# A four-mixer transformer on one core: orders changed in three stages, decays broadcast through DRAM, one product made transposed

## What is computed

```python
for l in range(2):                      # first block
    x = x + 0.5 * swiglu(rms_norm(x, ffa_norm[l]), ffa_w_in[l], ffa_w_out[l])
    h = rms_norm(x, mix_norm[l])
    (c_q, c_kv, k_rope, g_q, g_k, g_v, g_b, g_a, g_z, m_qkv, gate_logits) = split_cols(h @ w_in[l], IN_SPLITS)
    o_mla, o_gdn, o_moba = mla_branch(...), gdn_branch(...), moba_branch(...)
    x = x + gated sum of the branches @ w_out[l]
    x = x + 0.5 * swiglu(rms_norm(x, ffb_norm[l]), ffb_w_in[l], ffb_w_out[l])
# second block: even_mixer, ffn 0, odd mixer, ffn 1
```

```python
decay = jnp.exp(jnp.where(tril, gcum[..., :, None] - gcum[..., None, :], NEG_INF))
a  = jnp.where(strict, jnp.einsum('bhnid,bhnjd->bhnij', k_beta, k) * decay, 0.0)
qk = jnp.einsum('bhnid,bhnjd->bhnij', q, k) * decay
```

## Time and profile before

| | |
|---|---|
| median of 3 runs | 1898.7 us (1898.09 to 1899.29) |
| profiled execution | 1899.05 us |
| its span, first to last instruction | 1897.2 us |
| granted TensorE clock | 1.000 |
| busy: PE, DVE, ACT, POOL | 1888.0, 1460.1, 1083.3, 82.6 us |
| DMA | 330.87 MB, mean 174 GB/s |
| chain that ended last | PE 93%, DVE 4%, ACT 2% |

### The profile page before, as it was taken

One profiled execution on the slowest core, in us unless ns is written; L12 is line 12 of the kernel. 1 busy time (PEld: TensorE's weight loads), 2 busy tenths in 40 slices (PEclk: granted clock), 3 DMA queues, 4 the chain that ended last, 5 costly groups with the idle time before them and its releaser, 6 DMA issues.

```text
span 1897.2 us, 32403 instructions
## 1 busy us (share of the span) xinstructions
PE 1888.0 (100%) x11807; PEld 1649.0 (87%) x11807; DVE 1460.1 (77%) x2316; ACT 1083.3 (57%) x1683; POOL 82.6 (4%) x61
## 2 busy tenths in 40 slices
PE   9999999999999999999999999999999999999999
PEld 9888998788988888899987888889888889888888
DVE  7777896877777777778778777777578888888887
ACT  6555764664555555567647645555346655775654
POOL 0000011010000000000110010000000000110000
PEclk9999999999999999999999999999999999999999
DMA  6656553445455555555434455565755555545654
GB/s 236 199 189 197 171 188 102 134 152 170 155 190 188 187 186 190 188 183 185 155 112 145 145 172 179 186 197 180 207 179 178 198 189 173 162 143 158 200 186 143
DMA packets 116717, 330.87 MB, mean 174 GB/s; under 512 B 10896, under 2 KB 40208, under 8 KB 116496
## 3 DMA queue, kind: packets, MB, share of 16 engines
q1 hardware_dynamic: 114496, 325.64, 53.2%
q10 hardware_dynamic: 2128, 3.94, 0.6%
HBM read 327.91 MB, written 1.64 MB: 174 GB/s over the span
## 4 chain that ended last, share of the span: by engine, by line
PE 93%; DVE 4%; ACT 2%; DMA 1%; issue 0%; POOL 0%; ACTq 0%
PE ps L2318 89%; DVE w_lo L1319 1%; DMA raw<-stream 1%; PE ps L2344 1%; ACT w_hi L616 1%; PE ps L2617 1%; PE ps L2871 0%; DVE arena L2133 0%; DVE sc L1831 0%; PE ps L3035 0%; PE ps L2812 0%; PE ps L2893 0%; ACT gates L1113 0%; PE ps L2688 0%; DVE tmp L2176 0%
## 5 line engine op out<-in xcount | busy, mean ns | idle before, releaser
L1319 DVE TENSOR_TENSOR w_lo<-raw,w_hi 128x1024 fp32r<-128x1024 f32 x614 | 750.2, 1229 | 223.6 <-ACT w_hi L616 222.5
L2318 PE MATMUL ps<-w_hi,a_both 128*128 128x512 f32 (+2 forms) x2368 | 753.1, 387 | 1.1 <-DVE a_both L2105 0.7
L616 ACT ACTIVATE w_hi<-raw 128x1024 fp32r<-128x1024 f32 x614 | 637.2, 1053 | 160.8 <-DMA raw<-stream 106.0
L2318 PE MATMUL ps<-a_both,w_hi 128*128 128x256 f32 (+1 forms) x3360 | 712.4, 341 | 0.1
L2318 PEld LDWEIGHTS ps<-a_both,w_hi 128*128 128x128 f32 x3360 | 580.7, 190 | 72.8 <-issue 0.8
L2318 PEld LDWEIGHTS ps<-w_hi,a_both 128*128 128x128 f32 x2368 | 441.9, 188 | 88.6 <-issue 1.2
L2318 PE MATMUL ps<-w_lo,a_both 128*128 128x512 f32 (+2 forms) x1184 | 455.4, 385 | 0.0
L2318 PE MATMUL ps<-a_both,w_lo 128*128 128x256 f32 x2592 | 448.1, 283 | 0.0
L2318 PEld LDWEIGHTS ps<-a_both,w_lo 128*128 128x128 f32 x2592 | 380.5, 191 | 8.9
L2318 PEld LDWEIGHTS ps<-w_lo,a_both 128*128 128x128 f32 x1184 | 223.2, 188 | 36.5
L689 ACT ACTIVATE a_both<-arena 128x256 fp32r<-128x256 f32 x132 | 55.2, 419 | 139.4 <-DVE arena L1433 98.7
(11 more groups left out here) (349 smaller groups left out, 1186.7 us busy)
## 6 DMA issues: line engine op xcount, KB each, us to landing
raw<-stream SPq DMA_DIRECT2D x613, 512.0 KB, 3.5
arena<-upad SPq DMA_DIRECT2D x8, 284.0 KB, 6.0
gates<-late ACTq DMA_DIRECT2D x1, 1088.0 KB, 8.7
out<-tmp SPq DMA_DIRECT2D x3, 256.0 KB, 2.3
upad<-arena ACTq DMA_DIRECT2D x2, 288.0 KB, 8.1
con<-consts SPq DMA_DIRECT2D x1, 560.0 KB, 5.1
raw<-stream ACTq DMA_DIRECT2D x1, 512.0 KB, 3.8
x<-x_in ACTq DMA_DIRECT2D x2, 256.0 KB, 5.1
```

What stands on the lines that cost most here:

```text
L616: nc.scalar.activation(laid(w_hi, u), loaded(u), ACT.Copy).then_inc(hi_ready, 1)
L1319: V.tensor_tensor(laid(w_lo, u), loaded(u), laid(w_hi, u), ALU.subtract).then_inc(split_ready, 1)
L2318: return nc.tensor.matmul(o, a, b, start=start, stop=stop, **k)
```

## The change

Mixer, both layers: the running sums are stored to DRAM (1024 runs of 4 bytes) after load moba+1, and read back as 128 rows of 1024 after load moba+4, both on SP's queue; Et reads those rows. "R" is gone from PE. The product is made as K Q^T, masked by a second exponential ET (DVE adds a transposed mask after kgd, ACT takes eight exponentials with the negated sums as bias), so the transposition "QKT" and ACT's copy are gone. z_gate(1) stands between the two reductions, mobars after all of POOL's ATM steps. The constants grow by 128 columns of 1120.

```diff
+            def store_cum(l):
+                sp.wait_ge(*DV.at(l, "cumcp"))
+                sp.dma_start(cumd[l].rearrange("b p -> p b"), sc[:, 72:80], allow_slow_non_contiguous=True).then_inc(cum_stored, 16)
+            def spread_cum(l):
+                sp.wait_ge(cum_stored, 16 * (l + 1))
+                sp.dma_start(flat(rows), cumd[l].rearrange("b p -> (b p)").unsqueeze(0).broadcast_to([PART, 8 * PART])
+                             ).then_inc(cum_spread, 16)
...
+                        if u == POS["moba", l] + 1:
+                            store_cum(l)
+                        if u == POS["moba", l] + 4:
+                            spread_cum(l)
...
+                act.wait_ge(*DV.at(l, "ET"))
+                for b in range(8):
+                    e = nc.scalar.activation(ET[:, b, :], ET[:, b, :], ACT.Exp, bias=sc[:, 280 + b:281 + b])
+                e.then_inc(*AC.sig(l, "ET"))
                 turned_copy(0)
-                act.wait_ge(*PE.at(l, "QKT"))
-                nc.scalar.activation(QKT, ps[:, 4:6, :], ACT.Copy).then_inc(*AC.sig(l, "QKT"))
...
+                        tick(V.tensor_scalar(sc[:, 280:288], bank(6, 0, 8), -1.0, None, ALU.mult))
...
-                dve.wait_ge(*PE.at(l, "R"))
+                dve.wait_ge(cum_spread, 16 * (l + 1))
...
+                for t in range(2):
+                    i = V.tensor_tensor(ET[:, 4 * t:4 * t + 4, :], rows[:, 4 * t:4 * t + 4, :],
+                                        each(const("causalt"), 4), ALU.add)
...
-                ev(DV, "c_lo")
-                for b in range(8):
-                    i = mm(bank(6 + b // 4, 128 * (b % 4), 128 * (b % 4) + 128), sc[:, 240 + b:241 + b].broadcast_to([PART, 128]), const("tri"))
-                i.then_inc(*PE.sig(l, "R"))
...
-                blocks(4, lambda o, tt, h: mm(o, qT(tt, h), kT(tt, h)), "QK")
+                blocks(4, lambda o, tt, h: mm(o, kT(tt, h), qT(tt, h)), "QK")
...
-                ev(DV, "QK")
-                blocks(4, lambda o, tt, h: nc.tensor.transpose(o, QK[:, 4 * tt + h, :], ident), "QKT")
```

```diff
-                split(e0 + AHEAD); split(e0 + 1 + AHEAD)
+                split(e0 + AHEAD)
                 for p in range(2):
                     act.wait_ge(*DV2.at(0, f"yb{p}"))
...
-                split(e0 + 2 + AHEAD)
+                split(e0 + 1 + AHEAD)
...
-                dil_split(4, 5, 6, 7)
+                dil_split(4, 5)
+                nc.scalar.activation(sc[:, 300:301], sc[:, 296:297], ACT.Exp)
+                dil_split(6)
                 dil_evac(1)
                 squares("k", 2)
-                dil_split(8, 9, 10, 11)
+                dil_split(7, 8, 9, 10, 11)
...
+            for j in range(TT):
+                part = slice(DG * DH * j, DG * DH * (j + 1))
+                rsqrt(drs["k"][:, part], dss["k"][:, part]).then_inc(*PO2.sig(0, f"drsk{j}"))
...
                 tile(1, [n0 + 2, n0 + 3])
+                if n0 == POS["ffn", 0]:
+                    decay_rates()
                 with dve.Fori(0, (FT - 4) // 2) as j:
...
-                for i in range(4):
-                    scan = tick(V.tensor_tensor_scan(tqb[:, i, :], aa[:, i, :], thi[:, i, :], 0.0, ALU.mult, ALU.add))
-                dve.wait_ge(*PO2.at(0, "drsk"))
                 for j in range(TT):
+                    dve.wait_ge(*PO2.at(0, f"drsk{j}"))
                     r = dil["k"][:, j, :].rearrange("p (a b) -> p a b", b=DD)
                     e = V.tensor_tensor(r, r, over(drs["k"][:, 12 * j:12 * j + 12], DD), ALU.mult)
                 e.then_inc(*DV2.sig(0, "dk"))
+                for i in range(4):
+                    scan = tick(V.tensor_tensor_scan(tqb[:, i, :], aa[:, i, :], thi[:, i, :], 0.0, ALU.mult, ALU.add))
...
-                    update(t, POS["ffn", i] + 3 * FT, 1.0, ("mix2", 1))
+                    update(t, POS["ffn", i] + 3 * FT, 1.0, ("mix2", 1), between=POS["ffn", i] + 3 * FT - 3 + AHEAD)
```

More of the change, by code:

```diff
@@ L229, in constants @@
         neg += [same, band, same]
+    put("causalt", np.where(causal.T, 0.0, NEG).astype(np.float32))
     put("causal", np.where(causal, 0.0, NEG).astype(np.float32))
@@ L514, in build @@
         wcomp = gr(4592, 4 * TAP_STEP * TAP_GROUPS)
+        rows = reg(11264, 8, PART)
+        cumd = [nc.dram_tensor(f"cumd{l}", (8, PART), F32, kind="Internal").ap() for l in range(DEPTH)]
         upad = nc.dram_tensor("upad", (4 * PART, UPAD), F32, kind="Internal").ap()
@@ L588, in _ @@
                             spread_u(p)
+                    for l in range(DEPTH):
+                        if u == POS["moba", l] + 1:
+                            store_cum(l)
+                        if u == POS["moba", l] + 4:
+                            spread_cum(l)
             for b in range(2):
@@ L1026, in even @@
                 store_u(1)
+                act.wait_ge(*DV2.at(0, "lamz"))
+                link(nc.scalar.activation(sc[:, 288:292], sc[:, 284:288], ACT.Abs))
+                nc.scalar.activation(sc[:, 292:296], sc[:, 288:292], ACT.Exp, scale=-1.0).then_inc(*AC2.sig(0, "spe"))
                 def conv_out(p):
@@ L1067, in even @@
                                          ).then_inc(*AC2.sig(0, f"o2_hi{p}"))
-                for k in range(3, 8):
+                for k in range(2, 8):
                     split(e0 + k + AHEAD)
@@ L2097, in even @@
                 split(e0 + AHEAD)
-                split(e0 + 1 + AHEAD)
                 for p in range(2):
@@ L2106, in even, with decay_rates @@
                                     ALU.subtract).then_inc(*DV2.sig(0, f"o2_lo{p}"))
-                for k in range(2, 7):
+                for k in range(1, 7):
                     split(POS["ev_out"] + k + AHEAD)
+            def decay_rates():
+                dve.wait_ge(*AC2.at(0, "spe"))
+                sp = sc[:, 296:300]
+                log1p(sc[:, 292:296], sp, sc[:, 248:252], sc[:, 256:260], sc[:, 264:268])
+                link(V.scalar_tensor_tensor(sp, sc[:, 284:288], 0.0, sp, ALU.max, ALU.add))
+                V.tensor_scalar(sp, sp, -4.0, None, ALU.mult).then_inc(*DV2.sig(0, "sp4"))
             def odd(t):
```

65 lines of the change are left out of this document (33 added, 32 removed).

## The result

The changed kernel takes 1921.02 us (median of 4 runs, 1915.35 to 1921.32) against 1898.39 us before, measured beside it: ratio 1.0113, 95% interval [1.010, 1.0126]. The forecast was 1894.2 with a range of 1890.0 to 1897.3, so it had the wrong sign. The profiled execution took 1921.02 us with a span of 1919.2, 22.0 us more than before.

The account below looks back on a forecast made before the run. TensorE was taken as the bound, busy 1888.0 of 1897.2 us. Gains of 4.5 (mixer), 0.8 (even), 0.4 (ffn 0's end) and 0.5 (odd) less 1.7 (decay chain) made 4.5 us: 1894.2 us, range 1890.0 to 1897.3.

Parts of the forecast that it names:

- the price of the store: Mixer: the store of the decays to DRAM lands in about 4 us; at most 24.8 us if all cost is per run.
- its first 6.5 us are free: Mixer, SP's queue: source ready at 243.6, spread due near 250, so a store within some 6.5 us delays nothing.
- the slow rival: Mixer: SP waits for the store and holds later loads, DVE and kgd; 1907.2 us with a 14 us store; chance 0.05.
- The row I leaned on: Profile before: a 4 KB load of 128 short runs landed in 3.1 us; basis for the store's 4 us.
- 2.96 - s a layer: Mixer: 2.96 us of removed work and delay less s, PE's new stall for kgd, taken as 0.7 us.
- my signs of being wrong: No stall in ffn 0, both odd waits gone, or ACT waiting several us for loads in the mixer.
- The sentence on the Trainium skill: Mixer's store: runs below 512 bytes are slowest, which would move the sum from 1894.2 towards the rival's 1907.2.
- The mixer's gain, 4.5,: Both mixer layers: 2.25 us gained each, broadcast and transposes gone less a kgd stall; bounds 2.3 to 5.3 us.
- The even stage: Even stage: a weight split moved behind the output activation ends a 0.7 us stall; 0.8 us gained, bounds 0 to 0.9.
- The decay chain: Moved from odd stage to ffn 0's head: PE stalls 1.7 us for a weight split, a loss; bounds 0 to 2.0.
- ffn 0's end: End of ffn 0: x update before the split removes a 0.3 us stall; 0.4 us gained, bounds 0 to 0.5.
- The odd stage: Odd stage: keys scaled before the scans, 0.5 us gained for two stalls; bounds 1.0 lost to 2.9 gained.

Follow-up runs that it names:

- the store alone: Kernel before, with the store of 1024 runs of 4 bytes added on SP's queue and read by nobody: 1913.89 us, ratio 1.0089.
- on another queue (ACT's): Kernel before, with the unused store of 1,024 pieces of 4 bytes issued by ACT on its own DMA queue: 1917.72 us, ratio 1.0101.
- 1,024 pieces apart: Kernel before, with an unused store of all eight columns, each 4-byte piece 512 bytes from the next in DRAM: 1898.31 us, ratio 1.0004.
- the store of one column: Kernel before, with an unused store of one of the 8 columns, 128 pieces of 4 bytes, on SP's queue: 1910.60 us, ratio 1.0064.
- the kernel with 128 runs: The change, with the sums stored in 128 runs of 32 bytes and DVE reading rows with a stride of eight values: 1897.86 us, ratio 1.000.
- the last kernel: The change with 8 stored rows of 512 bytes, decay chain back in odd stage, even stage's last split after x update: 1893.96 us, ratio 0.9981.

## Why the prediction was wrong

**The step that failed** is the price of the store, and with it the reckoning that its first 6.5 us are free. I took 4 us for its landing, "nearest to that row, since a plain load of 512 KB takes 3.5 us too", and gave the slow rival 0.05. It landed in 9.8 and 11.3 us, by the spread that waits for it. The row I leaned on the earlier trace rows was a load of 128 short runs that reads DRAM; a store of short pieces that fill the same stretch is another thing, and no row before had one. My upper bound, eight times that row (24.8 us), was right as a bound but reckoned by the number of runs, and the runs show that the number is not what counts.

**The rival's mechanism was half right.** Its chain, late loads, then DVE, then PE, is what the trace shows. But I let it begin at SP, which waits in order, and so took 6.5 us as free: only the load behind the spread would be late. In fact the three loads issued right after the store were late, with SP free (the store alone) and on another queue (ACT's). So nothing was free. By my rule, 2.96 - s a layer, a store of 10 us gives s of about 3 and no loss; PE's stalls were 6.3 and 8.0 us, start to start, and with the clock the layers lost 8.5 and 12.3 us. In my terms s was 11.4 and 15.2, where I took 0.7. Of my signs of being wrong it was the last that came: ACT waited 10.4 us for a load.

**The sentence on the Trainium skill** (DMA: Bandwidth & Descriptors, Specifications) pointed to the right side: below 512 bytes a run the engine reads, modifies and writes. It does not say by itself why 1,024 pieces apart land in 3.1 us and 128 side by side in 7.9, all of 4 bytes. Read, modify and write of the same stretch by many pieces would fit that difference, but the runs show only the times.

**The clock** was in none of my cases, so I had put it at nothing: all of before ran at the full grant. By the estimate above it added about 12 us (5.1 and 7.2), twice what the removed work of both mixers saves.

**The mixer's gain, 4.5,** came out near once the store is written in rows: 4.2 and 4.3 in the two kernels that do so, with no wait for kgd in layer 0 and 0.6 in layer 1, where I took 0.7 for each. That it is so near is partly luck: making the rows costs PE 0.4 us a layer, so the rest gains 5.1, close to my upper bound of 5.3. That the spread is "as large as one weight load" and mostly harmless held: it landed in 4.9 us there.

**The even stage failed:** forecast +0.8, in the change -0.6. The stall at line 2105 went, but "I give the postponed ones room enough" was wrong. A postponed split stands right ahead of the update of x on DVE, and PE waited 1.3 us for x. The four other kernels with this order lose 0.2 to 2.7 us there in their profiles. With that split behind the update the stage gains 0.5.

**The decay chain was right:** forecast 1.7 lost, 1.9 in the change, 1.8 when put back; the new stall is where I put it, a weight split at the loop's head.

**ffn 0's end** gained 0.7 in the profile, a little over my bound of 0.5; 0.4 was forecast. **The odd stage** is 1.2 to 1.6 us shorter in the profiles where I took 0.5, but no gain is shown: my two stalls, 1.5 and 1.2 us, came from one execution, and the same code is as short without the edit in others. The power function in two halves cost what I took (5.58 us for two, 2.8 each):

```profile
1672.74 5.58 POOL L1258 TENSOR_TENSOR sc<-sc,nhalf 128x12 f32<-128x12 f32 x2 [47.58 <-DVE sc L2209]
```

The key transposes' wait is gone in all seven kernels with the new order, as forecast. The one for the weights' transposes (line 3071) is 0.6 us where I expected it to grow, and a new one of 0.8 us waits for ACT's copies (line 1119), for which I had no term.

## What to carry to other kernels

Before a small tensor is sent through DRAM to change its layout, look at which addresses the pieces of the store hit, not only at how many there are. In these runs, where 128 to 1,024 pieces of 4 bytes filled 512-byte stretches, the loads issued behind them landed in 9.5 to 14.3 us (medians of a few loads) in place of 4.1, on another queue too. Put the layout change on an engine first (here one small product and a copy) and store whole rows. When a kernel's TensorE is hardly ever idle, a stall of several us can cost more than its length: in the change the clock took about as much again, with the store alone nothing in layer 0. And before a stall of 1 us is priced from one profile, see whether other executions of the same code show it.

## What was not expected of the hardware

- 128 stores of 4 bytes into one 512-byte stretch landed in 7.4 to 8.4 us, and the loads behind them in 9.8 to 10.1 in place of 4.1, loads on another queue too (13.0, with 1,024 of them); 1,024 stores each 512 bytes apart landed in 2.9 to 3.4 us, with loads at 4.5 to 4.6 and no stall of PE in the mixers.
- The granted clock does not follow the length of the stalls alone. With the store alone PE stood 1.9, 1.3 and 2.4 us in layer 0, start to start, and windows from 240 to 290 all show 1.00. With the store of one column it stood only 1.3 and 2.4 us at the same place, and the clock fell. The same ten microseconds, store alone and then one column (PE is busy for the same time; the clock is 1.00 and 0.83):

```profile
260.00:270.00 10.00, 6.54 (x28) 4.86 (x29) 10.00 (x20) 8.67 (x16) 0.00 (x0) 1.00 0.45 160
```

```profile
260.00:270.00 10.00, 6.54 (x29) 5.38 (x28) 10.00 (x20) 7.97 (x13) 0.00 (x0) 0.83 0.42 144
```

  In the change it stood 1.7, 1.3 and 3.2 us, and the clock fell to 0.50. Why it fell in one and not in the other is open.
- DVE reading SBUF with a stride of eight values: the operation that writes E took 1.14 us in the kernel with 128 runs and 0.69 in the last kernel, where it reads in a row, by the trace of its line in each (kernel with 128 runs first; min/median/max in ns):

```profile
L1804 DVE SCALAR_TENSOR_TENSOR gates<-arena,con x4: 1128/1138/1155, 266.5 to 916.1; 128x512 f32<-128x512 f32 x4
```

```profile
L1802 DVE SCALAR_TENSOR_TENSOR gates<-arena,con x4: 685/690/696, 266.2 to 914.4; 128x512 f32<-128x512 f32 x4
```

  Two of these a layer stand ahead of kgd, 0.9 us. The wait for kgd in layer 1 was 2.0 us longer there than with rows (2.6 against 0.6); the other 1.1 us is not explained.
